# Two 256-token matmuls per weight tile in place of one of 512, in the gate and up projections of a two-block network

## The chip, the cores and the metric

The kernel runs on one core of one Trainium2 chip. The metric is the device time of one execution in microseconds (us); the median of three runs of the kernel before is 2926.17 us (2924.74 to 2929.9).

## The reference, cut to what matters

The reference is a two-block network on 512 tokens of width 1024, in fp32: feed-forward, a hybrid mixer (state-space and banded attention), feed-forward; then a gated-delta-rule mixer, feed-forward, a gated projection, a stick-breaking attention, feed-forward, a gated projection. The change touches the first two products of each of the four feed-forward layers:

```
D_MODEL, SEQ, D_FF = 1024, 512, 2816

def swiglu(h, w_gate, w_up, w_down):
    return (jax.nn.silu(h @ w_gate) * (h @ w_up)) @ w_down

# first block, twice (around its mixer)
x = x + 0.5 * swiglu(rms_norm(x, ffn_norm), w_gate, w_up, w_down)
# second block, twice (gate and up are the halves of one matrix)
h = h + swiglu_2(rms_norm_2(h, ln_ffn), ffn_w_in, ffn_w_out)
```

## The kernel before

Activations are kept transposed: features lie on the 128 partitions, the 512 tokens (T) along the free dimension, so x is 8 tiles (DK) of 128 x 512. Each fp32 product is made of three matmuls on operands split into a high and a low part of type fp32r: high weights by high x, high weights by low x, low weights by high x. The fourth, low by low, is left out.

Weights come in units of 128 x 1024. For a gate or up layer a unit holds the 8 weight tiles (128 x 128) that give one output tile of 128 features by 512 tokens. SyncE's queue loads the units one after another into `raw` (2 slots, L1787), ScalarE rounds each into `w_hi` (4 slots, L392), GpSimd subtracts to get `w_lo` (L1822), and TensorE uses it.

The code of the feed-forward layers on TensorE is `pe_ffn`. The 22 tiles of hidden features go in two halves of 12 and 10. For each half, `pe_column_layer` runs 24 or 20 units (gate and up in turn), each with 24 matmuls (L326 to L328, k over 8, three for each k) into one PSUM bank of 512 fp32 columns; then `pe_square_half` runs twice for the down projection (L351 to L353). So the gate and up projections are 44 units a feed-forward layer and 176 in all, 4224 matmuls. The same `pe_column_layer` also makes the mixers' projections, which share lines L326 to L328 but not the change: 2256 more matmuls.

The order of work is the program's: each engine runs its own list and waits on counting semaphores. A unit waits once, at its first matmul, for `w_lo` of the unit and for a free bank. In the first unit of a layer (j == 0) each k also waits for its `x_lo` tile, which VectorE writes (L418). `each` writes the first unit out, runs a loop of laps of four units with a jump back (L118), and writes the last ones out: with 24 units 1 + 5 laps of 4 + 3, with 20 units 1 + 4 laps of 4 + 3.

While a unit runs, VectorE takes the result of the unit before out of PSUM with the scale (L495, L497), makes the product with the activated gate (L500) and its low part (L502). ScalarE does the SiLU (L467) and `mid_hi` (L470).

A matmul instruction of fp32r shows in the trace as one weight load (LDWEIGHTS, engine PEld) and one matmul (MATMUL, PE). A matmul on plain fp32 operands, as the mixers have them, shows as two of each, called passes below.

Of the kernel before, what the change touches and what calls it, by code (L numbers as in the profile page):

```python
# [24 lines left out]
T = 512  # L25
NB = T // P
D = 1024
DK = D // P
# [80 lines left out]
def each(eng, count, body, first=0, begin=0):  # L109

    at, end = begin + first, begin + count
    for u in range(begin, at):
        body(0, u)
    laps = (end - at) // 4
    if laps >= 2:
        with eng.Fori(0, laps) as i:  # L118
            for j in range(at, at + 4):
                body(i, j)  # L120
        at += laps * 4
    for u in range(at, end):
        body(0, u)
# [41 lines left out]
def build(nc, units, x_t, p_t, vectors, constants, rel_table, out_t):  # L165
# [4 lines left out]
    def place(name, at, shape, dtype=F32):  # L170

        size = int(np.prod(shape[1:])) * 4
        assert base + at + size <= limit, (name, base + at + size, limit)
        return nc.alloc_sbuf_tensor_at(name, shape, dtype, offset=base + at)

    with ExitStack() as ctx:
# [8 lines left out]
        x_hi = place("x_hi", 56 * KB, [P, DK, T], F32R)  # L185
        x_lo = place("x_lo", 72 * KB, [P, DK, T], F32R)
# [87 lines left out]
        ps = ctx.enter_context(nc.psum_tensor("ps", [P, 8, T], F32))  # L274
# [34 lines left out]
        def pe_norm_sum(pe, w, bank):  # L309

            pe.wait_ge(s_sum, 8 * (w.norms + 1))
            nc.tensor.matmul(ps[:, bank, :], ones, sum_sq[:, :], start=True, stop=True).then_inc(s_msum, 1)

        def pe_column_layer(pe, w, count, after_first=None):
            n0, b0, g = w.column_layer(count)

            def body(i, j):
                u, slot = i * 4 + j, (n0 + j) % W_SLOTS
                pe.wait_ge(s_wlo, n0 + u + 1)
                pe.wait_ge(s_free, b0 + u + 1)  # L320
                for k in range(DK):
                    if j == 0:
                        pe.wait_ge(s_xlo, w.tiles - DK + k + 1)
                    hi, lo = w_hi[:, slot, k * P:(k + 1) * P], w_lo[:, slot, k * P:(k + 1) * P]
                    out = ps[:, 4 * g + j % 4, :]
                    nc.tensor.matmul(out, hi, x_hi[:, k, :], start=(k == 0), stop=False)  # L326
                    nc.tensor.matmul(out, hi, x_lo[:, k, :], start=False, stop=False)  # L327
                    last = nc.tensor.matmul(out, lo, x_hi[:, k, :], start=False, stop=(k == DK - 1))  # L328
                last.then_inc(s_used, 1)
                if j == 0 and after_first is not None:  # L330
                    after_first(4 * (g ^ 1))

            each(pe, count, body, first=1)

        def pe_square_half(pe, w, tiles, rhs, ready):

            n0, b0, g, prev, _ = w.square_layer(tiles // 2)
            for kp in range(tiles // 2):
                slot = (n0 + kp) % W_SLOTS
                pe.wait_ge(s_wlo, n0 + kp + 1)  # L340
                if kp == 0:
                    pe.wait_ge(s_free, prev + 4)
                for k2 in range(2):
                    k = 2 * kp + k2
                    ready(k)
                    r_hi, r_lo = rhs(k)
                    for m in range(4):
                        at = k2 * T + m * P
                        hi, lo = w_hi[:, slot, at:at + P], w_lo[:, slot, at:at + P]
                        out = ps[:, 4 * g + m, :]  # L350
                        nc.tensor.matmul(out, hi, r_hi, start=(k == 0), stop=False)  # L351
                        nc.tensor.matmul(out, hi, r_lo, start=False, stop=False)  # L352
                        last = nc.tensor.matmul(out, lo, r_hi, start=False, stop=(k == tiles - 1))  # L353
                        if k == tiles - 1 and m < 3:
                            last.then_inc(s_bank, 1)
                last.then_inc(s_used, 1)
# [82 lines left out]
        def pe_ffn(pe, w):  # L439
            for half, tiles in enumerate(HALVES):  # L440
                if half == 0:
                    w.tiles += DK
                    pe_column_layer(pe, w, 2 * tiles, lambda bank: pe_norm_sum(pe, w, bank))
                    w.norms += 1
                else:
                    pe_column_layer(pe, w, 2 * tiles)
                mids = w.mids
                for side in range(2):
                    pe_square_half(pe, w, tiles, lambda k: (mid_hi[:, k, :], mid_lo[:, k, :]),
                                   lambda k: pe.wait_ge(s_mlo, mids + k + 1))  # L450
                w.mids += tiles
# [183 lines left out]
        def pe_mixer1(pe, w):  # L635
            w.tiles += DK
            pe_column_layer(pe, w, U_END, lambda bank: pe_norm_sum(pe, w, bank))
            w.norms += 1
            pe_rstd_columns(pe, w)
# [1221 lines left out]
        @block.tensor  # L1861
        def _(pe):
            w = Walk()
            pe.wait_ge(s_const2, 16)
            pe_ffn(pe, w)
            pe_mixer1(pe, w)
            pe_ffn(pe, w)
            pe_final_norm(pe, w)
            pe_mixer2(pe, w)
            pe_ffn(pe, w)  # L1870
            pe_embed(pe, w)
            pe_mixer3(pe, w)
            pe_ffn(pe, w)
            pe_embed(pe, w)
            assert w.unit == NREAL, (w.unit, NREAL)
# [130 lines left out]
```

## Time and profile before

| | |
|---|---|
| median of 3 runs | 2926.17 us |
| lowest, highest | 2924.74, 2929.9 us |
| span of the profiled execution | 2923.0 us |
| weight loads and matmuls recorded | 12450 each |
| mean granted TensorE clock | 0.969 |

The profiled execution has no time of its own beside its span (first to last instruction). The median of the runs lies 3.2 us above that span; this is taken as what lies around it.

How to read the rows: the time shown for a matmul is from its start to its modelled end, and matmuls overlap, so neither the sum of durations nor the busy share tells the rate. The rate is the distance from one start to the next; it is called the pitch below.

### The profile page before, as it was taken

The page shows a single profiled execution, that of the slowest core. Times are in us where ns is not written, and L with a number is a line of the kernel's source. Part 1 is how long each engine was busy: PE and PEld are TensorE (multiplying, and loading weights), DVE is VectorE, ACT ScalarE, POOL GpSimd, SP SyncE. Part 2 cuts the span into 40 slices and gives each one's busy share as a digit, 9 for nine tenths or more (in the row PEclk, how much of TensorE's full clock was granted, in tenths as well). Part 3 has the DMA queues.
Part 4 walks back from the last instruction along what each step waited for, and adds up shares of the span by engine and source line. Part 5 has one row for each costly group of instructions (what it writes and reads, how often), then busy time and mean ns, then how long its engine had stood idle before and what let it go on. Part 6 is the DMA issues. An engine that isn't in the chain of part 4 may idle for free.

```text
span 2923.0 us, 35055 instructions
## 1 busy us (share of the span) xinstructions
PE 2758.2 (94%) x12450; PEld 2197.1 (75%) x12450; DVE 995.6 (34%) x1504; ACT 1029.6 (35%) x1475; POOL 1103.4 (38%) x522
## 2 busy tenths in 40 slices
PE   8999999979899999899888899999999989999998
PEld 6888888644788888676577678888778567888886
DVE  3212228347332121884433352112241322321224
ACT  4222333334342222424543442222342443422233
POOL 4444434300344444344322234444344402444443
PEclk9999999989999999999898999999999999999999
DMA  4333322300233333123000023333223101333333
GB/s 150 93 101 94 97 90 88 107 0 1 72 94 94 101 93 101 58 87 100 0 0 0 0 86 95 100 96 99 87 85 90 49 0 43 101 94 101 94 101 101
DMA packets 61691, 222.27 MB, mean 76 GB/s; under 512 B 6704, under 2 KB 6832, under 8 KB 61488
## 3 DMA queue, kind: packets, MB, share of 16 engines
q1 hardware_dynamic: 60928, 218.07, 24.5%
q10 hardware_dynamic: 688, 3.15, 0.3%
q8 instruction: 53, 0.87, 0.1%
q14 instruction: 22, 0.18, 0.0%
HBM read 219.09 MB, written 2.10 MB: 76 GB/s over the span
## 4 chain that ended last, share of the span: by engine, by line
PE 67%; issue 19%; POOL 7%; ACT 3%; DVE 3%; DMA 0%; POOLq 0%; ACTq 0%; SPq 0%; DVEq 0%
PE ps L326 12%; PE ps L328 12%; PE ps L327 12%; POOL w_lo L1822 7%; PE ps L351 5%; PE ps L352 5%; PE ps L353 5%; PE ps L1240 2%; PE ps L1605 2%; PE ps L1231 1%; PE ps L589 1%; PE ps L1092 1%; PE ps L372 1%; PE ps L374 1%; PE ps L373 1%
## 5 line engine op out<-in xcount | busy, mean ns | idle before, releaser
L1822 POOL TENSOR_TENSOR w_lo<-raw,w_hi 128x1024 fp32r<-128x1024 f32 x405 | 988.5, 2442 | 1436.6 <-ACT w_hi L392 1436.5
L326 PE MATMUL ps<-x_hi,w_hi 128*128 128x512 f32 x2160 | 850.4, 394 | 32.6 <-DVE x_lo L418 16.9
L328 PE MATMUL ps<-x_hi,w_lo 128*128 128x512 f32 x2160 | 842.6, 390 | 0.0
L327 PE MATMUL ps<-x_lo,w_hi 128*128 128x512 f32 x2160 | 842.6, 390 | 0.0
L392 ACT ACTIVATE w_hi<-raw 128x1024 fp32r<-128x1024 f32 x405 | 425.4, 1051 | 578.0 <-PE ps L353 360.7
L326 PEld LDWEIGHTS ps<-x_hi,w_hi 128*128 128x128 f32 x2160 | 406.7, 188 | 132.5 <-issue 26.7
L328 PEld LDWEIGHTS ps<-x_hi,w_lo 128*128 128x128 f32 x2160 | 406.6, 188 | 85.6
L327 PEld LDWEIGHTS ps<-x_lo,w_hi 128*128 128x128 f32 x2160 | 406.9, 188 | 85.2 <-issue 2.2
L351 PE MATMUL ps<-mid_hi,w_hi 128*128 128x512 f32 x960 | 377.4, 393 | 21.9 <-DVE mid_lo L1536 13.1
L352 PE MATMUL ps<-mid_lo,w_hi 128*128 128x512 f32 x960 | 375.8, 391 | 0.0
L353 PE MATMUL ps<-mid_hi,w_lo 128*128 128x512 f32 x960 | 375.5, 391 | 0.0
L517 DVE SCALAR_TENSOR_TENSOR h<-ps,h 128x512 f32<-128x512 f32 x88 | 60.2, 689 | 497.9 <-PE ps L353 497.9
L351 PEld LDWEIGHTS ps<-mid_hi,w_hi 128*128 128x128 f32 x960 | 181.9, 189 | 61.7 <-issue 24.0
L352 PEld LDWEIGHTS ps<-mid_lo,w_hi 128*128 128x128 f32 x960 | 181.8, 189 | 38.3 <-issue 0.5
L353 PEld LDWEIGHTS ps<-mid_hi,w_lo 128*128 128x128 f32 x960 | 181.6, 189 | 38.2
L497 DVE TENSOR_TENSOR ff_up<-ps,rstd 128x512 f32<-128x512 f32 x88 | 60.9, 692 | 406.9 <-PE ps L328 406.9
L470 ACT ACTIVATE mid_hi<-ff_up 128x512 f32 (+1 forms) x88 | 55.6, 632 | 390.7 <-DVE ff_up L500 390.7
L629 DVE SCALAR_TENSOR_TENSOR cv<-pad,vec,cv 128x512 f32<-128x512 f32 x108 | 146.1, 1353 | 15.7 <-DVE cv L629 0.3
L467 ACT ACTIVATE ff_gate<-ff_gate 128x512 f32<-128x512 f32 x88 | 55.6, 632 | 252.8 <-DVE ff_gate L495 252.7
L495 DVE TENSOR_TENSOR ff_gate<-ps,rstd 128x512 f32<-128x512 f32 x88 | 60.9, 692 | 223.6 <-PE ps L328 205.3
L1491 POOL TENSOR_TENSOR ao<-at,const 128x512 f32<-128x512 f32 x48 | 60.4, 1271 | 163.0 <-DVE tt L1435 111.5
L502 DVE TENSOR_TENSOR mid_lo<-ff_up,mid_hi 128x512 f32 x88 | 65.8, 748 | 80.9 <-ACT mid_hi L470 80.9
(268 smaller groups left out, 2456.8 us busy)
## 6 DMA issues: line engine op xcount, KB each, us to landing
raw<-in_units_dram SPq DMA_DIRECT2D x406, 512.0 KB, 3.6
h<-in_x_t_dram SPq DMA_DIRECT2D x4, 512.0 KB, 6.8
toep<-in_rel_table_dram ACTq DMA_DIRECT2D x1, 2048.0 KB, 9.1
out_dram<-h SPq DMA_DIRECT2D x4, 512.0 KB, 5.5
p_f<-in_p_t_dram ACTq DMA_DIRECT2D x2, 512.0 KB, 3.8
const<-in_constants_dram SPq DMA_DIRECT2D x1, 832.0 KB, 9.5
vec<-in_vectors_dram SPq DMA_DIRECT2D x1, 133.5 KB, 2.3
```

The source lines that it names most:

```text
L326: nc.tensor.matmul(out, hi, x_hi[:, k, :], start=(k == 0), stop=False)
L327: nc.tensor.matmul(out, hi, x_lo[:, k, :], start=False, stop=False)
L328: last = nc.tensor.matmul(out, lo, x_hi[:, k, :], start=False, stop=(k == DK - 1))
L351: nc.tensor.matmul(out, hi, r_hi, start=(k == 0), stop=False)
L352: nc.tensor.matmul(out, hi, r_lo, start=False, stop=False)
L353: last = nc.tensor.matmul(out, lo, r_hi, start=False, stop=(k == tiles - 1))
L392: nc.scalar.activation(w_hi[:, n % W_SLOTS, :], raw[:, n % RAW_SLOTS, :], ACT.Copy).then_inc(s_whi, 1)
L495: nc.vector.tensor_tensor(ff_gate[:, pair, :], ps[:, 4 * g + j % 4, :], rstd[:, :], ALU.mult).then_inc(s_free, 1)
L497: nc.vector.tensor_tensor(ff_up[:, pair, :], ps[:, 4 * g + j % 4, :], rstd[:, :], ALU.mult).then_inc(s_free, 1)
L502: nc.vector.tensor_tensor(tile_at(mid_lo, done), ff_up[:, pair, :], tile_at(mid_hi, done).bitcast(F32), ALU.subtract).then_inc(s_mlo, 1)
L629: last = nc.vector.scalar_tensor_tensor(out=cv[:, slot, :], in0=pad[:, slot, q:q + T], scalar=tap(q), in1=cv[:, slot, :], op0=ALU.mult, op ...
L1822: nc.gpsimd.tensor_tensor(w_lo[:, n % W_SLOTS, :], raw[:, n % RAW_SLOTS, :], w_hi[:, n % W_SLOTS, :].bitcast(F32), ALU.subtract).then_inc( ...
```

## The change

In `pe_column_layer`, where the new argument `token_halves` is true, a weight tile's three matmuls of 512 tokens become two sets of three matmuls of 256 tokens, the first on tokens 0 to 255 and the second on 256 to 511. Both write the same PSUM bank, each its own half. Only the very first matmul of a bank carries the start flag. `pe_ffn` passes true for both halves of all four feed-forward layers. No other engine's list changes.

```diff
-        def pe_column_layer(pe, w, count, after_first=None):
+        def pe_column_layer(pe, w, count, after_first=None, token_halves=False):
...
-                    out = ps[:, 4 * g + j % 4, :]
-                    nc.tensor.matmul(out, hi, x_hi[:, k, :], start=(k == 0), stop=False)
-                    nc.tensor.matmul(out, hi, x_lo[:, k, :], start=False, stop=False)
-                    last = nc.tensor.matmul(out, lo, x_hi[:, k, :], start=False, stop=(k == DK - 1))
+                    if not token_halves:
...
+                    else:
+                        for t in range(2):
+                            cols = slice(t * T // 2, (t + 1) * T // 2)
+                            out = ps[:, 4 * g + j % 4, cols]
+                            nc.tensor.matmul(out, hi, x_hi[:, k, cols], start=(k == 0 and t == 0), stop=False, skip_group_check=True)
+                            nc.tensor.matmul(out, hi, x_lo[:, k, cols], start=False, stop=False, skip_group_check=True)
+                            last = nc.tensor.matmul(out, lo, x_hi[:, k, cols], start=False, stop=(k == DK - 1), skip_group_check=True)
...
-                    pe_column_layer(pe, w, 2 * tiles, lambda bank: pe_norm_sum(pe, w, bank))
+                    pe_column_layer(pe, w, 2 * tiles, lambda bank: pe_norm_sum(pe, w, bank), True)
...
-                    pe_column_layer(pe, w, 2 * tiles)
+                    pe_column_layer(pe, w, 2 * tiles, None, True)
```

On TensorE, the first unit of the first feed-forward layer, k = 0 and the start of k = 1. Before:

```order
L326 MATMUL ps<-x_hi,w_hi 128x512 [waits banks_free,x_lo_ready,w_lo_ready,masks_loaded]
L327 MATMUL ps<-x_lo,w_hi 128x512
L328 MATMUL ps<-x_hi,w_lo 128x512
L326 MATMUL ps<-x_hi,w_hi 128x512 [waits x_lo_ready]
L327 MATMUL ps<-x_lo,w_hi 128x512
```

After:

```order
L334 MATMUL ps<-x_hi,w_hi 128x256 [waits banks_free,x_lo_ready,w_lo_ready,masks_loaded]
L335 MATMUL ps<-x_lo,w_hi 128x256
L336 MATMUL ps<-x_hi,w_lo 128x256
L334 MATMUL ps<-x_hi,w_hi 128x256
L335 MATMUL ps<-x_lo,w_hi 128x256
L336 MATMUL ps<-x_hi,w_lo 128x256
L334 MATMUL ps<-x_hi,w_hi 128x256 [waits x_lo_ready]
```

Between one wait for an `x_lo` tile and the next there were three matmuls, and there are six of half the width.

On TensorE, the end of a unit inside the loop and the start of the next (L319 counts the wait's value). Before:

```order
L326 MATMUL ps<-x_hi,w_hi 128x512
L327 MATMUL ps<-x_lo,w_hi 128x512
L328 MATMUL ps<-x_hi,w_lo 128x512
L319 REGISTER_ALU
L326 MATMUL ps<-x_hi,w_hi 128x512 [waits banks_free,w_lo_ready]
```

After:

```order
L334 MATMUL ps<-x_hi,w_hi 128x256
L335 MATMUL ps<-x_lo,w_hi 128x256
L336 MATMUL ps<-x_hi,w_lo 128x256
L319 REGISTER_ALU
L334 MATMUL ps<-x_hi,w_hi 128x256 [waits banks_free,w_lo_ready]
```

The waits stand at the same places; from one to the next there are 48 matmuls in place of 24, so a loop's body is 192 in place of 96.

## Rows read from the trace of the kernel before

**Rows 1.** The page: busy time, share of the span, instructions of each engine; granted clock.

```profile
span 2923.0 us, 35055 instructions
PE 2758.2 (94%) x12450; PEld 2197.1 (75%) x12450; DVE 995.6 (34%) x1504; ACT 1029.6 (35%) x1475; POOL 1103.4 (38%) x522
```

**Rows 2.** Windows: a gate-and-up layer of 20 units; busy us by engine.

```profile
core 0: us, PE busy (x) PEld busy (x) DVE busy (x) ACT busy (x) POOL busy (x), PEclk, DMA share, GB/s
1008.60:1117.40 108.80, 108.80 (x482) 90.09 (x481) 26.60 (x39) 31.12 (x39) 47.97 (x20) 1.00 0.31 96
```

**Rows 3.** Groups of the page: count, busy us, mean ns, idle time before and its releaser.

```profile
L326 PE MATMUL ps<-x_hi,w_hi 128*128 128x512 f32 x2160 | 850.4, 394 | 32.6 <-DVE x_lo L418 16.9
L328 PE MATMUL ps<-x_hi,w_lo 128*128 128x512 f32 x2160 | 842.6, 390 | 0.0
L326 PEld LDWEIGHTS ps<-x_hi,w_hi 128*128 128x128 f32 x2160 | 406.7, 188 | 132.5 <-issue 26.7
```

**Rows 4.** Timeline, a steady stretch of such a layer: start us, duration us, engine.

```profile
249.93 0.39 PE L327 MATMUL ps<-x_lo,w_hi 128*128 128x512 f32 x1
...
251.06 0.39 PE L326 MATMUL ps<-x_hi,w_hi 128*128 128x512 f32 x1
...
249.93 0.19 PEld L328 LDWEIGHTS ps<-x_hi,w_lo 128*128 128x128 f32 x1
250.16 0.19 PEld L326 LDWEIGHTS ps<-x_hi,w_hi 128*128 128x128 f32 x1
```

**Rows 5.** Timeline, the kernel's first matmuls, at the lower granted clock.

```profile
14.30 0.63 PE L328 MATMUL ps<-x_hi,w_lo 128*128 128x512 f32 x1
14.73 0.63 PE L326 MATMUL ps<-x_hi,w_hi 128*128 128x512 f32 x1
15.16 0.63 PE L327 MATMUL ps<-x_lo,w_hi 128*128 128x512 f32 x1
```

**Rows 6.** Timeline, mixers: plain fp32 passes of 384, 128, 256 and 512 columns.

```profile
2356.03 0.81 PE L1615 MATMUL ps<-sb_l,sb_v 128*128 128x384 f32 x2
2356.68 0.38 PE L1613 MATMUL ps<-sb_l,sb_v 128*128 128x128 f32 x2
2356.90 0.60 PE L1615 MATMUL ps<-sb_l,sb_v 128*128 128x256 f32 x2
2357.34 0.38 PE L1613 MATMUL ps<-sb_l,sb_v 128*128 128x128 f32 x2
...
1669.29 7.03 PE L1092 MATMUL ps<-nrm_sq,const 128*128 128x512 f32 x16
```

**Rows 7.** Timeline, weight loads of a stream of 128-column passes.

```profile
1473.09 0.30 PEld L1269 LDWEIGHTS ps<-qkt,vn 128*128 128x128 f32 x2
1473.32 0.30 PEld L1271 LDWEIGHTS ps<-vn,kd 128*128 128x128 f32 x2
1473.54 0.30 PEld L1267 LDWEIGHTS ps<-qd,st 128*128 128x128 f32 x2
```

**Rows 8.** Timeline, two of eight small transposes in a row, one instruction each.

```profile
643.75 0.21 PE L696 MATMUL ps<-const,cs_row 16*128 16x16 f32 x1
643.81 0.21 PE L697 MATMUL ps<-const,dt_row 16*128 16x16 f32 x1
```

**Rows 9.** Loads of one lap of the delta-rule loop; DMA queues from 1465 to 1680 us.

```profile
1486.00:1542.00 56.00, 45.41 (x374) 0.96 0.00 0
...
DMA packets 1, 0.01 MB, mean 0 GB/s; under 512 B 0, under 2 KB 0, under 8 KB 0
q14 instruction: 1, 0.01, 0.0%
```

**Rows 10.** First unit of a layer: TensorE's wait for x_lo; line L418's own durations.

```profile
816.59 0.50 PE L326 MATMUL ps<-x_hi,w_hi 128*128 128x512 f32 x1 [0.30 <-DVE x_lo L418]
L418 DVE SCALAR_TENSOR_TENSOR x_lo<-h,vec,x_hi x80: 735/747/2241, 8.2 to 2857.8; 128x512 fp32r<-128x512 f32 x80
```

More of the change, by code:

```diff
@@ L324, in body @@
                     hi, lo = w_hi[:, slot, k * P:(k + 1) * P], w_lo[:, slot, k * P:(k + 1) * P]
-                    out = ps[:, 4 * g + j % 4, :]
-                    nc.tensor.matmul(out, hi, x_hi[:, k, :], start=(k == 0), stop=False)
-                    nc.tensor.matmul(out, hi, x_lo[:, k, :], start=False, stop=False)
-                    last = nc.tensor.matmul(out, lo, x_hi[:, k, :], start=False, stop=(k == DK - 1))
+                    if not token_halves:
+                        out = ps[:, 4 * g + j % 4, :]
+                        nc.tensor.matmul(out, hi, x_hi[:, k, :], start=(k == 0), stop=False)
+                        nc.tensor.matmul(out, hi, x_lo[:, k, :], start=False, stop=False)
+                        last = nc.tensor.matmul(out, lo, x_hi[:, k, :], start=False, stop=(k == DK - 1))
+                    else:
[5 more added lines that the diff above has]
+                            last = nc.tensor.matmul(out, lo, x_hi[:, k, cols], start=False, stop=(k == DK - 1), skip_group_check=True)
                 last.then_inc(s_used, 1)
```

## The prediction

> **What bounds the kernel now.** I read the page first: TensorE is busy for 94% of the span, no other engine for more than 38% [rows 1]. A busy share of pipelined matmuls is not a rate, so the windows come next, cut to the layers that the change touches. A layer of 20 units holds 480 matmuls and takes 108.8 us, with TensorE busy in all of it, and the granted clock is 1.00, the 2.4 GHz level [rows 2]: 226.7 ns from start to start, 5.44 us a unit. The timeline shows the same in single rows: five matmuls from 249.93 to 251.06, 226 ns each [rows 4]. In that layer GpSimd, the busiest helper, works 48.0 us and ScalarE 31.1 us of 108.8 [rows 2], so weights are ready long before they are needed. In the groups, all 2160 matmuls of L326 are preceded by 32.6 us of idle time together, and L328 by none [rows 3]. TensorE's own pace sets the time here, and a nanosecond added to each matmul's pitch is a nanosecond on the end.
>
> **What a pitch is made of.** At 2.4 GHz one column per cycle, 512 columns are 213.3 ns. The pitch is 226.7, so 13.3 ns are something else. Three readings bear on what.
> - At the lower clock (0.5, 1.2 GHz) the same matmuls start 0.43 us apart [rows 5], and 512 columns are 426.7 ns there: nothing is left over. So the 13.3 ns are no gap in issuing that would show at either clock.
> - Plain fp32 passes run at 1.2 columns per ns. Two of 384 columns take 0.65 us (0.325 each, 320 for the columns), two of 256 take 0.44 (0.22; 213), two of 128 take 0.22 (0.11; 107), and sixteen of 512 take 7.03 us with the last one's drain, where their columns are 6.83, so at most 12 ns each are left [rows 6]. What is left of the narrower ones is 3 to 7 ns by rows rounded to 10 ns. One column in 17 lost would be 20 ns at 384 and 27 at 512: a part per pass, not a rate.
> - Each matmul has a weight load, which starts when the matmul before it starts and is shown as 0.19 us long [rows 4].
>
> **The change part by part.**
>
> *Columns.* 4224 matmuls of 512 become 8448 of 256: the same number of columns. At one column per cycle this part costs nothing.
>
> *The part per matmul.* If the 13.3 ns are paid once for each matmul and its load, a matmul of 256 has a pitch of 106.7 + 13.3 = 120.0 ns. The gate and up layers take 8448 x 120.0 = 1013.8 us in place of 4224 x 226.7 = 957.4: +56.3 us. Before has no fp32r matmul narrower than 512, so this cost must be bounded. Below: if the 13.3 ns are a rate (one column in 17 lost), 256 columns take 113.3 ns and the change costs nothing; and if they go altogether, the next limit is the weight load. Loads of 128 columns start 0.22 us apart for two, that is 111 to 112 ns [rows 7]; 8448 x 111.7 = 943.6 us, -13.8 us. Above: if the 13.3 ns come on top of the load's own 111.7, the pitch is 125.0 and the cost +98.6 us. I take 120.0, because the plain fp32 rows, the nearest with several widths, have a remainder that is the same at every width, and because the load is the same size at each width: whatever it takes from the moving operand, it takes once a load.
>
> *The loads.* They double, from 4224 to 8448. Today a load has 226.7 ns to hide in, in future about 120. The row at issue is the shown length, 188 ns [rows 3], longer than the new pitch. But loads of 0.19 us each follow each other every 0.11 us under the 128-column passes, two of them within 0.30 [rows 7]. So the shown length is latency, loads overlap each other, and the cover of 120 ns is enough, by 8 ns. That margin is thin, and it is why the range goes up to the case above.
>
> The Trainium skill's page "Perfetto Trace Analysis", section "Identifying the Most-Contended Engine", advises judging TensorE by LDWEIGHTS busy share, summed slice time over the window. By that rule the layer of 20 units is at 90.1 of 108.8 us, 83%, and doubled loads want 180 us: the load would become the bound. The trace speaks against it, since 374 loads of 0.19 us, 71 us by their sum, stood in 45.4 us of busy time within one lap of the delta-rule loop [rows 9].
>
> *Issuing.* Twice as many instructions go through TensorE's sequencer in the same time, one every 120 ns. Small transposes, one instruction each, start 0.06 us apart [rows 8], so issuing hides with a factor of two.
>
> *The loop's body.* It grows from 96 to 192 load-and-matmul pairs. The delta-rule loop's laps have 374 loads, and over its second to fourth lap TensorE's instruction queue moves nothing (the one packet is of q14, another queue) [rows 9]. A body twice as long as the new one is held, so a jump back costs nothing.
>
> The skill's page "Runtime: NRT & Kernel Launch", section "Instruction fetch mechanics", says that a taken branch beyond a window of two pages of code forces a fetch. The same row speaks against it for a body of this size.
>
> *The first units.* There each k waits for x_lo, which VectorE makes in some 0.75 us a tile, and TensorE idles, 0.30 us in the case shown [rows 10]. Six matmuls of 120.0 take 0.72 us where three took 0.68, so part of the 0.32 us that a first unit grows by is taken from this idle time: at most 1.3 us over four layers, which I leave at 0.5 given back. The kernel's first matmuls run at the lower clock, where two of 256 should take what one of 512 takes, since nothing is left over there [rows 5].
>
> *Other engines and memory.* Nothing is added on VectorE, ScalarE, GpSimd or SyncE. A unit lengthens from 5.44 to 5.76 us, which gives them slack. Three matmuls running add onto the same 256 columns, 120 ns apart; the two passes of a 128-column product add onto the same columns 110 ns apart without a stall [rows 6]. The bank is released after the unit's last matmul, as before.
>
> *Sum.* 2923.0 + 56.3 - 0.5 = 2978.8 us of span; with 3.2 us around it, by the distance of the median from this span, 2982.0 us, +1.9%.
>
> **The rivals.**
>
> *The extra is a rate, or goes (not slower).* Pitch 113.3 down to 111.7: 2926 down to 2912 us. For it: the lower clock shows no extra at all [rows 5], as would be if the moving operand's supply were just short of 2.4 columns per ns; that is a rate. Against it: a shortage of supply would also be expected from a load that shares it, which is once per load. The point at which it decides is a pitch of 113.3; below it the kernel is faster than before, and it is faster by over 0.2% only below 112.6.
>
> *Part of it is a rate (slower, less).* The plain passes pay 3 to 7 ns each whatever their width; if fp32r pays 3 of that kind and the other 10.3 are a rate, 256 columns have 106.7 + 5.2 + 3 = 114.9 ns, +13 us, 2939 us. For it, that the plain passes, with the same loads, pay no more; against it, that a load then costs fp32r nothing beyond what it costs them.
>
> The skill's page "TensorE: Matmul & The Clock Gate", section "Back-to-back issue gap", gives 262 cycles for 256 columns and 518 for 512, 109.2 and 215.8 ns at 2.4 GHz, so the change would add 11 us by it, close to this rival. The trace disagrees on 512 columns, 226.7 ns.
>
> *The load becomes the bound (slower).* The 107 ns of columns no longer cover a load of 111.7 ns, and the 13.3 come on top: 125.0 ns, 2926.2 + 98.6 = 3025 us. For it: the margin is 8 ns, and no row shows loads this dense beside a moving operand at full rate. Against: then loads would have to be slowed by what slows the matmul.
>
> *Loads don't overlap with fp32r* (188 ns each as shown): 8448 x 188 = 1588 us, +631, 3557 us. Against it rows 7, though those are passes of plain fp32.
>
> *The narrow matmul loses the full rate* and runs as plain fp32 does, 216 ns for 256: 1825 us, +867, 3794 us. Nothing in the trace shows it, nor excludes it.
>
> *Code is fetched again at each jump back.* There are 28 of them (four layers by 4 + 3). The waits put down to issue before L326's loads are 26.7 us in all [rows 3]; as many again would give 3009 us. Against it rows 9.
>
> **How the numbers follow.** Chances: forecast 0.54; extra is a rate or goes 0.15 (0.06 of it under 2920); part of it a rate 0.08; load as the bound 0.12; code fetch 0.03; loads in full 0.04; full rate lost 0.04. The range goes from 2920 to 3040 us: from the rate case up to a pitch of 126.8. It leaves out the two large cases and the lower end of the first rival. A measurement of this kernel can tell 0.2% from no change, 6 us, a pitch of 112.6 to 114.0. Faster 0.06, same 0.09, slower 0.85.
>
> **What would show it.** In the profile after, a layer of 20 units should take 115.2 us where it took 108.8 and hold 960 loads, with starts 120 ns apart in the timeline. The remainder after 106.7 ns is the answer: 13.3 for the forecast, 6.6 for a rate, 8.2 for part of it a rate, 18 for the load as the bound, 81 for loads in full. A load's shown length should stay near 0.19 us. The down projections should keep 226.7 ns, and the instruction queue should have no more packets during the loops. Idle time before the first matmul of a unit, once in each lap, would mean code fetch. If the clock row falls below 1.00 in these layers, or GpSimd's w_lo shows as a releaser there, the prediction's basis is wrong.

## The result and the profile after

The changed kernel takes 2982.81 us (median of 4 runs, 2979.36 to 2985.56), the kernel before 2927.94 in the same measurement; the ratio on record is 1.0192, with a 95% interval of 1.0175 to 1.021 (the two medians by themselves give 1.0187). The profiled execution has a span of 2977.5 us, 54.5 more than before. The page of the changed kernel, with the gate and up matmuls now on L334 to L336:

```profile
span 2977.5 us, 43503 instructions
PE 2812.8 (94%) x16674; PEld 2418.7 (81%) x16674; DVE 999.3 (34%) x1504; ACT 1029.8 (35%) x1475; POOL 1103.6 (37%) x522
...
q8 instruction: 65, 1.06, 0.1%
...
L334 PE MATMUL ps<-x_hi,w_hi 128*128 128x256 f32 x2816 | 799.6, 284 | 13.9 <-DMA const<-in_constants_dram 13.2
L335 PE MATMUL ps<-x_lo,w_hi 128*128 128x256 f32 x2816 | 797.4, 283 | 0.0
```

There are 16674 - 12450 = 4224 more matmuls, as many as were cut in two, and TensorE waits before L334 for 13.9 us in all, 13.2 of it for the first load of constants, and before L335 for nothing. Its busy share is 94% as before, so this share says nothing about the pace.

The windows of the changed kernel, a layer of 24 units and one of 20 (answering to [rows 2]):

```profile
core 0: us, PE busy (x) PEld busy (x) DVE busy (x) ACT busy (x) POOL busy (x), PEclk, DMA share, GB/s
824.60:964.30 139.70, 139.46 (x1156) 138.74 (x1156) 39.43 (x55) 46.30 (x59) 57.58 (x24) 1.00 0.27 90
1029.50:1144.80 115.30, 115.30 (x962) 115.26 (x961) 26.55 (x39) 31.10 (x39) 48.01 (x20) 1.00 0.27 91
```

The layer of 20 units went from 108.8 to 115.2 us, taken from its first start to the first start behind it (the window is 0.1 longer), with the clock at 1.00 in both, and DVE, ACT and POOL do the same work in it. Its 960 matmuls and loads are 120 ns apart, as the timeline (answering to [rows 4]; start us, duration us, engine) shows row by row:

```profile
1080.05 0.28 PE L335 MATMUL ps<-x_lo,w_hi 128*128 128x256 f32 x1
1080.17 0.28 PE L336 MATMUL ps<-x_hi,w_lo 128*128 128x256 f32 x1
1080.29 0.28 PE L334 MATMUL ps<-x_hi,w_hi 128*128 128x256 f32 x1
...
1080.05 0.19 PEld L336 LDWEIGHTS ps<-x_hi,w_lo 128*128 128x128 f32 x1
1080.17 0.19 PEld L334 LDWEIGHTS ps<-x_hi,w_hi 128*128 128x128 f32 x1
```

256 columns at 2.4 per ns are 106.7 ns, so 13.3 ns are left, exactly what was left of 226.7 at 512 columns. The loads, 0.19 us long, now overlap each other (PEld busy 115.26 of 115.30 us), and that does no harm.

### The profile page after: what moved, and what is told of

Read it like the earlier page. It is cut to its first block, busy times and chain, and to the rows that moved or that the text cites. A ratio compares the mean times of both kernels' runs of the same rounds, so it can differ in the third digit from the quotient of the medians.

```text
span 2977.5 us, 43503 instructions
## 1 busy us (share of the span) xinstructions
PE 2812.8 (94%) x16674; PEld 2418.7 (81%) x16674; DVE 999.3 (34%) x1504; ACT 1029.8 (35%) x1475; POOL 1103.6 (37%) x522
## 4 chain that ended last, share of the span: by engine, by line
PE 67%; issue 19%; POOL 6%; DVE 3%; ACT 3%; DMA 0%; POOLq 0%; SPq 0%; ACTq 0%; DVEq 0%
PE ps L334 8%; PE ps L336 8%; PE ps L335 8%; POOL w_lo L1830 6%; PE ps L359 5%; PE ps L360 5%; PE ps L361 5%; PE ps L327 4%; PE ps L329 4%; PE ps L328 4%; PE ps L1248 2%; PE ps L1613 2%; PE ps L1239 1%; PE ps L597 1%; PE ps L1100 1%
## 5 line engine op out<-in xcount | busy, mean ns | idle before, releaser
L334 PE MATMUL ps<-x_hi,w_hi 128*128 128x256 f32 x2816 | 799.6, 284 | 13.9 <-DMA const<-in_constants_dram 13.2
L335 PE MATMUL ps<-x_lo,w_hi 128*128 128x256 f32 x2816 | 797.4, 283 | 0.0
L336 PE MATMUL ps<-x_hi,w_lo 128*128 128x256 f32 x2816 | 797.4, 283 | 0.0
L334 PEld LDWEIGHTS ps<-x_hi,w_hi 128*128 128x128 f32 x2816 | 541.2, 192 | 15.8 <-DMA const<-in_constants_dram 13.2
L335 PEld LDWEIGHTS ps<-x_lo,w_hi 128*128 128x128 f32 x2816 | 541.3, 192 | 1.2 <-issue 1.0
L336 PEld LDWEIGHTS ps<-x_hi,w_lo 128*128 128x128 f32 x2816 | 541.1, 192 | 0.0
L327 PE MATMUL ps<-x_hi,w_hi 128*128 128x512 f32 x752 | 299.5, 398 | 18.3 <-DVE x_lo L426 15.9
L328 PE MATMUL ps<-x_lo,w_hi 128*128 128x512 f32 x752 | 294.3, 391 | 0.0
L329 PE MATMUL ps<-x_hi,w_lo 128*128 128x512 f32 x752 | 294.2, 391 | 0.0
L327 PEld LDWEIGHTS ps<-x_hi,w_hi 128*128 128x128 f32 x752 | 142.1, 189 | 60.7 <-issue 25.7
L329 PEld LDWEIGHTS ps<-x_hi,w_lo 128*128 128x128 f32 x752 | 142.1, 189 | 30.0
```

Of the source, the lines that this page charges most:

```text
L334: nc.tensor.matmul(out, hi, x_hi[:, k, cols], start=(k == 0 and t == 0), stop=False, skip_group_check=True)
L335: nc.tensor.matmul(out, hi, x_lo[:, k, cols], start=False, stop=False, skip_group_check=True)
L336: last = nc.tensor.matmul(out, lo, x_hi[:, k, cols], start=False, stop=(k == DK - 1), skip_group_check=True)
```

## The experiments

The rows fixed the size of the cost at once. Open was whether it is what the sum took it for, one part per matmul, and when the weight load takes over. Edits are against the changed kernel. "Before" in each text is the kernel before.

**Half of the layers.** A dose and a test of even spread.

```diff
-                    pe_column_layer(pe, w, 2 * tiles, None, True)
+                    pe_column_layer(pe, w, 2 * tiles)
```

> The gate and up layers of 24 units use 256-token matmuls, those of 20 units keep 512. Theory (13.3 ns once for each fp32r matmul and its load, pitch 120.0): 96 units of 24 matmuls split, 2304 x (240.0 - 226.7) = +30.7 us over the kernel before, ratio 1.0105; the 24-unit layers' unit 5.76 us, the 20-unit layers' 5.44 us. Rival (something paid once for each layer, stage or jump back, such as code fetch or a late wait, that only happens to sum to 56 us): by jumps back 16 of 28, +32 us, but then as gaps in the timeline and not as an even pitch; by layers, half, +28 us.

Measured: 2958.95 us against 2925.39 for the kernel before on the same chip, ratio 1.0107 (1.009 to 1.0124), where 1.0105 was expected. The windows, a layer of 24 units and one of 20:

```profile
core 0: us, PE busy (x), PEclk, DMA share, GB/s
824.20:964.00 139.80, 139.55 (x1157) 1.00 0.28 90
1029.30:1138.20 108.90, 108.90 (x482) 1.00 0.30 96
```

The split layer has the changed kernel's time and the other has that of before, so the cost sits inside the split layers. The total can't tell the two theories apart (+30.7 or +28 to +32 us): by the medians it grew by 33.6 us, and the four runs lie from 2952.55 to 2960.85. The pitch does: the starts in the split layers are 120.0 ns apart, and no gap recurs at the laps. The rival of something paid per lap or per layer falls.

**The same weight twice in a row.** Is the part for exchanging one tile for another?

```diff
-                        for t in range(2):
-                            cols = slice(t * T // 2, (t + 1) * T // 2)
-                            out = ps[:, 4 * g + j % 4, cols]
-                            nc.tensor.matmul(out, hi, x_hi[:, k, cols], ...)
-                            nc.tensor.matmul(out, hi, x_lo[:, k, cols], ...)
-                            last = nc.tensor.matmul(out, lo, x_hi[:, k, cols], ...)
+                        halves = [slice(t * T // 2, (t + 1) * T // 2) for t in range(2)]
+                        bank = 4 * g + j % 4
+                        for t, cols in enumerate(halves):
+                            nc.tensor.matmul(ps[:, bank, cols], hi, x_hi[:, k, cols], ...)
+                        for cols in halves:
+                            nc.tensor.matmul(ps[:, bank, cols], hi, x_lo[:, k, cols], ...)
+                        for cols in halves:
+                            last = nc.tensor.matmul(ps[:, bank, cols], lo, x_hi[:, k, cols], ...)
```

> Halves as in the changed kernel, but the two token halves of one weight tile stand directly behind each other (high by x_hi on both halves, high by x_lo on both, low by x_hi on both), so each load but the first of a pair brings what the array already holds. Theory (once per matmul, whatever is loaded): pitch 120.0 everywhere, the time of the changed kernel, 2982 us, ratio to before 1.019. Rival (the part is for exchanging one weight tile for another): the second of each pair costs 2.5 to 3 ns in place of 13.3, so 4224 x 10.8 = 45 us are given back, ratio 1.004.

Measured: 2982.12 us, ratio 1.0194 (1.0177 to 1.0211). Timeline, two matmuls to a row:

```profile
1080.05 0.40 PE L336 MATMUL ps<-x_lo,w_hi 128*128 128x256 f32 x2
1080.29 0.40 PE L338 MATMUL ps<-x_hi,w_lo 128*128 128x256 f32 x2
```

0.24 us for two, with a load for each (the page of this run has 16674 loads, as many as matmuls). Whether a load brings a new tile or the same one doesn't matter, and the order within a k neither.

**The down projections too.** Does the part hold in a layer with another order of banks?

```diff
-                        out = ps[:, 4 * g + m, :]
-                        nc.tensor.matmul(out, hi, r_hi, start=(k == 0), stop=False)
...
+                        for t in range(2):
+                            cols = slice(t * T // 2, (t + 1) * T // 2)
+                            out = ps[:, 4 * g + m, cols]
+                            nc.tensor.matmul(out, hi, r_hi[:, cols], start=(k == 0 and t == 0), stop=False, skip_group_check=True)
...
```

> The down projections of the four feed-forward layers, and the mixers' output projections made by the same function, use 256-token matmuls too: 2880 more matmuls of 512 become 5760 of 256. Theory: 2880 x 13.3 = +38.4 us over the changed kernel, 2927.9 + 56.3 + 38.4 - 0.5 = 3022 us, ratio 1.0322. Rival (the 120 ns belong to the column layers alone, where one bank is written for 48 matmuls; the down projection goes round four banks): nothing added, 1.019, or another pitch, up to the load-bound 125, 1.042.

Measured: 3017.84 us, ratio 1.0316 (1.0299 to 1.0333). Over the changed kernel that is 35.0 us by the medians and 37.1 by the spans of the profiled executions (3014.6 and 2977.5), where 38.4 were expected. The two down projections behind a layer of 20 units in a window of this kernel:

```profile
1162.00:1219.60 57.60, 57.60 (x482) 1.00 0.31 94
```

Their 480 matmuls take 57.5 us from first start to last: the pitch is the same 120. The rival that the 120 ns belong to the column layers falls. In the two traces the stretches that were split here grew by 37.9 us together, 0.5 less than 38.4. The rest of what is missing lies within the spread of the runs, 2 us for this kernel and 6 us for the changed one.

**Quarters.** Where does the load become the bound? The slice is a quarter, and t runs over four.

```diff
-                        for t in range(2):
-                            cols = slice(t * T // 2, (t + 1) * T // 2)
+                        cuts = (0, 128, 256, 384, 512)
+                        for t in range(len(cuts) - 1):
+                            cols = slice(cuts[t], cuts[t + 1])
```

> Each weight tile is used for four sets of matmuls of 128 tokens in the gate and up layers, 16896 matmuls in place of 4224. This asks where the weight load becomes the bound. Theory (13.3 per matmul on the columns' time, loads beside it with a floor of 111.7 as the plain passes show): 53.3 + 13.3 = 66.7 is below the floor, so pitch 111.7, 16896 x 111.7 = 1887 us for the layers, +930 us, 3857 us. Rival (the part comes on top of whichever is longer): pitch 125, +1154 us, 4082 us. Rival (loads go faster when the matmul does): pitch 66.7 to 111, from +169 us, 3097 us.

Measured: 3862.87 us (one run) against the 3857 of the theory. A window over a layer of 20 units:

```profile
1376.70:1591.10 214.40, 214.40 (x1922) 214.39 (x1920) 26.51 (x39) 31.05 (x39) 47.44 (x20) 1.00 0.17 51
```

214.4 us for 1920 matmuls is 111.7 ns each, with 53.3 ns of columns in it. This is the pace at which loads follow each other in [rows 7] too. The 13.3 ns don't come on top of it, so the rival of 125 ns falls. In the changed kernel the 120 ns lie above this floor. That the floor is the load's is a reading. For it, the next experiment has loads 0.11 us apart where two matmuls start 0.06 apart. It is no floor of every 4-byte load of 128 columns: those of the small transposes, on 16 partitions, follow each other faster in the kernel before (their matmuls are in [rows 8]), and are shown shorter:

```profile
643.78 0.14 PEld L697 LDWEIGHTS ps<-const,dt_row 16*128 16x128 f32 x1
643.84 0.14 PEld L696 LDWEIGHTS ps<-const,cs_row 16*128 16x128 f32 x1
```

**Unequal parts.** 384 tokens, then 128, by `cuts = (0, 384, 512)`.

> Each weight tile is used for 384 tokens and then for 128, in the gate and up layers. Theory (pitch is the columns' time plus 13.3, or the floor that a weight load sets, 111.7, where that is longer): 384 columns 160 + 13.3 = 173.3, 128 columns 111.7, together 285.0 for what took 226.7, 4224 x 58.3 = +246 us, 3174 us. Rival (the matmul's and the load's parts trade off over several matmuls, since loads run ahead during the wide ones): 173.3 + 66.7 = 240, the same time as the changed kernel, 2982 us. The matmul behind which the long pitch stands tells in which one's time the load lies.

Measured: 3178.19 us (one run), where 3174 was expected. The timeline of one k:

```profile
1199.92 0.39 PE L335 MATMUL ps<-x_hi,w_hi 128*128 128x384 f32 x1
1200.15 0.34 PE L336 MATMUL ps<-x_lo,w_hi 128*128 128x384 f32 x1
1200.32 0.34 PE L337 MATMUL ps<-x_hi,w_lo 128*128 128x384 f32 x1
1200.50 0.22 PE L335 MATMUL ps<-x_hi,w_hi 128*128 128x128 f32 x1
1200.56 0.27 PE L336 MATMUL ps<-x_lo,w_hi 128*128 128x128 f32 x1
1200.67 0.27 PE L337 MATMUL ps<-x_hi,w_lo 128*128 128x128 f32 x1
1200.78 0.40 PE L335 MATMUL ps<-x_hi,w_hi 128*128 128x384 f32 x1
...
1200.33 0.19 PEld L335 LDWEIGHTS ps<-x_hi,w_hi 128*128 128x128 f32 x1
1200.50 0.19 PEld L336 LDWEIGHTS ps<-x_lo,w_hi 128*128 128x128 f32 x1
1200.61 0.19 PEld L337 LDWEIGHTS ps<-x_hi,w_lo 128*128 128x128 f32 x1
1200.72 0.19 PEld L335 LDWEIGHTS ps<-x_hi,w_hi 128*128 128x128 f32 x1
1200.83 0.19 PEld L336 LDWEIGHTS ps<-x_lo,w_hi 128*128 128x128 f32 x1
```

Six matmuls take 0.86 us (0.855 expected), so the part and the floor are not averaged over several matmuls, and the rival of 240 ns for a pair falls. The single rows need care. The load of the first narrow matmul starts at 1200.33, beside the last wide one. The load of the second starts only with the first, at 1200.50, and still the second is shown 0.06 later. But it is shown as 0.27 us long, where the first is 0.22, and the 384 at 1200.78 as 0.40 in place of 0.34. So it seems that a matmul whose load is late is shown from before the load is in, and that the wait is part of its shown time; then the gaps of 0.06 and 0.23 are not costs of their own. In the rows a load never starts earlier than the matmul before its own.

**Narrower loads.** Is the part a share of the load's columns? Here the matmuls have 512 tokens again.

```diff
...
+                        out = ps[:, 4 * g + j % 4, :]
+                        nc.tensor.matmul(out, hi, x_hi[:, k, :], start=(k == 0), stop=False, skip_group_check=True)
+                        nc.tensor.matmul(out[0:64], hi[:, 0:64], x_lo[:, k, :], start=False, stop=False, skip_group_check=True)
+                        last = nc.tensor.matmul(out[0:32], lo[:, 0:32], x_hi[:, k, :], start=False, stop=(k == DK - 1), skip_group_check=True)
```

> 512-token matmuls as in the kernel before, but in the gate and up layers the second product (high by x_lo) is made for 64 of the 128 features of a tile only and the third (low by x_hi) for 32; the low parts of the others are left out. So the weight loads of a k are 128, 64 and 32 columns wide. Theory A (the 13.3 ns are taken by the load from the moving operand in proportion to the columns loaded): the matmul beside the 64-column load is at 213.3 + 2.5 + 5.4, beside the 32-column one at 213.3 + 2.5 + 2.7, 16 ns less a k, 1408 x 13.5 = -19 us against before. Theory B (fixed per load or matmul whatever its width): 226.7 throughout, the time of before.

Measured: 2939.44 us (one run) against 2929.59 of before, slower than either theory. Timeline:

```profile
1050.24 0.39 PE L332 MATMUL ps<-x_hi,w_hi 128*128 128x512 f32 x1
1050.47 0.39 PE L333 MATMUL ps<-x_lo,w_hi 128*64 128x512 f32 x1
1050.70 0.40 PE L334 MATMUL ps<-x_hi,w_lo 128*32 128x512 f32 x1
1050.93 0.39 PE L332 MATMUL ps<-x_hi,w_hi 128*128 128x512 f32 x1
...
1050.24 0.14 PEld L333 LDWEIGHTS ps<-x_lo,w_hi 128*64 128x64 f32 x1
1050.47 0.11 PEld L334 LDWEIGHTS ps<-x_hi,w_lo 128*32 128x32 f32 x1
```

The loads are shown shorter (0.14, 0.11 us), but all starts are 0.23 apart, 231 ns on average in place of 226.7. So a shorter load gives nothing back, which speaks against the load taking turns with the moving operand column by column. (The pitches that the text above gives for theory A save 13.6 ns a k, not 16.) The two matmuls with narrower loads also write fewer partitions of PSUM, so two things changed at once, and why this costs 4 ns more a matmul is open.

**Two readings with bf16.** Both operands of the gate and up matmuls are read as the upper 16 bits of the same tiles, a stride of 4 bytes.

```diff
+                        def top(ap):
+                            return ap.bitcast(mybir.dt.bfloat16)[:, 1::2]
...
+                        nc.tensor.matmul(out, top(hi), top(x_hi[:, k, :]), start=(k == 0), stop=False)
...
```

> 512-token matmuls as in the kernel before, but in the gate and up layers both operands are read as the upper 16 bits of the same tiles, as bf16; the lower bits of the operands are left out. Theory (the 13.3 ns belong to 4-byte operands at the full column rate): pitch 213.3 + about 2.5 = 216, as the remainder of the plain passes, 4224 x -10.8 = -46 us against before, 2882 us. Rival (once per load and matmul whatever the type): 226.7, 2928 us.

> The same bf16 reading (lower bits left out) with 256-token matmuls. Theory (types decide the part): 106.7 + 2.5 = 109.2 if the load keeps up, 8448 x 109.2 = 922 us for the layers, -35 us against before, 2893 us; 111.7 if a load of 128 columns is still the floor, -14 us. Rival (once per load and matmul whatever the type): 120.0, 2983 us.

Measured: 2922.91 and 2929.77 us (one run each) against 2929.59. At 512 the starts are 225.0 ns apart, at 256 113.3, so neither theory holds: what is left beside the columns, 11.7 and 6.7 ns, grows with the width. In this form the halves are almost free, 1.7 ns a pair, where fp32r pays 13.3.

**All widths.** Each of the eight gate-and-up layers is a stream of one width of fp32r; a table replaces the halves.

```diff
+        LAYERS = [(512, (0,)), (448, (0, 64)), (384, (0, 128)), (320, (0, 192)), (288, (0, 224)), (256, (0, 256)), (240, (0, 136, 272)), (224, (0, 144, 288))]
...
+                        width, starts = kind
+                        for t, at in enumerate(starts):
+                            cols = slice(at, at + width)
```

> The eight gate-and-up layers, in the order in which they run, use fp32r matmuls of 512, 448, 384, 320, 288, 256, 240 and 224 tokens, in one, two or three sets that together cover the 512 tokens; where sets overlap, tokens are added twice, so the values there are not the reference's. Each layer is thus a stream of one width. Theory (columns at 2.4 per ns plus 13.3 ns a matmul, not under the load's floor of 111.6 that the 128-token run showed): pitches 226.7, 200.0, 173.3, 146.7, 133.3, 120.0, 113.3, 111.6; +331 us against before, 3259 us. Rival (the part is a rate, one column in 17, and the 120.0 at 256 is the load's doing): 226.7, 198.3, 170.0, 141.7, 127.5, 120.0, 111.6 to 120, 111.6 to 120; +311 us or more, 3239 us.

Measured: 3257.99 us (one run); the theory had 3259. The windows from the layer of 448 to that of 224:

```profile
213.20:407.80 194.60, 194.60 (x961) 180.34 (x961) 26.54 (x39) 31.11 (x39) 47.99 (x20) 1.00 0.17 57
899.20:1099.60 200.40, 200.40 (x1155) 199.92 (x1154) 37.01 (x55) 46.03 (x58) 57.33 (x24) 1.00 0.20 65
1164.90:1305.70 140.80, 140.80 (x961) 140.76 (x960) 26.53 (x39) 31.11 (x39) 48.27 (x20) 1.00 0.23 76
1917.70:2072.10 154.40, 154.40 (x1156) 153.92 (x1155) 38.69 (x55) 46.10 (x59) 57.61 (x24) 1.00 0.26 85
2137.40:2252.60 115.20, 115.20 (x962) 115.20 (x961) 26.50 (x39) 31.30 (x39) 47.92 (x20) 1.00 0.27 90
2709.70:2905.20 195.50, 195.50 (x1732) 194.98 (x1732) 37.17 (x55) 46.22 (x59) 57.38 (x24) 1.00 0.21 69
2970.50:3131.30 160.80, 160.80 (x1442) 160.80 (x1441) 26.47 (x39) 31.15 (x39) 47.79 (x20) 1.00 0.21 69
```

| columns | matmuls | pitch measured, ns | columns' time, ns | left, ns |
|---|---|---|---|---|
| 448 | 960 | 202.7 | 186.7 | 16.0 |
| 384 | 1152 | 173.3 | 160.0 | 13.3 |
| 320 | 960 | 146.7 | 133.3 | 13.3 |
| 288 | 1152 | 133.3 | 120.0 | 13.3 |
| 256 | 960 | 120.0 | 106.7 | 13.3 |
| 240 | 1728 | 112.6 | 100.0 | 12.6 |
| 224 | 1440 | 111.7 | 93.3 | 18.4 |

The pitch is the mean distance between starts within the layer, the first unit aside. At 256, 288, 320, 384 and 512 columns the same 13.3 ns are left: a part per matmul. A rate would have left 10.0 at 384 and 7.5 at 288. At 224 the load's floor of 111.7 is reached. Two widths don't fit: 240 takes 0.7 ns less than the 113.3 of the theory, and 448 takes 2.7 ns more than its 200.0. Both are unexplained. In the total they partly cancel (2.6 us more, 1.3 us less), so its agreement within 1 us is closer than the theory deserves.

**Which operand bf16 pays for.** The eight layers differ in what is packed (2 bytes from element to element): both operands, the moving one alone, or the load alone. Packed operands come from a constant tile.

```diff
+        LAYERS = [("bf16", "packed", "packed", 512), ("bf16", "packed", "packed", 256), ("bf16", "packed", "strided", 512), ("bf16", "packed", "strided", 256), ("bf16", "strided", "packed", 512), ("bf16", "strided", "packed", 256), ("bf16", "packed", "packed", 128), ("bf16", "packed", "strided", 128)]
...
+                        dtype, moving, loaded, width = kind
```

> The gate-and-up layers read bf16 operands, in the order: moving operand packed (2 bytes from one element to the next, from a constant tile) with a packed load, 512 and 256 columns; moving packed with the load taken at a stride of 4 bytes from the weights, 512 and 256; moving operand at a stride of 4 bytes from x with a packed load, 512 and 256; moving packed, 128 columns, packed load, then strided load. The products of these layers are thereby replaced by others of the same shapes. Known before: strided both, 225.0 at 512 and 113.3 at 256, so 225.0 = 213.3 + 11.7 and 113.3 = 106.7 + 6.7. Theory (the remainder comes from reading 4 bytes a column at the full rate on the moving side): packed moving 215.8 and 109.2 whatever the load is, strided moving 225.0 and 113.3. Rival (it comes from the load's reading): packed load 215.8 and 109.2 whatever the moving operand is, strided load 225.0 and 113.3. At 128 columns a load's shown 0.10 us in place of 0.19 should let the pitch fall under 111.6, to between 56 and 96.

Measured: 2903.2 us (one run) against 2926.15. The windows (weight loads) with the moving operand packed and the load strided, 256 columns; moving strided and load packed, 256; moving packed and load strided, 128:

```profile
core 0: us, PEld busy (x), PEclk, DMA share, GB/s
994.60:1099.50 104.90, 93.94 (x961) 1.00 0.30 100
1909.20:2018.10 108.90, 91.89 (x962) 1.00 0.29 96
2669.80:2777.10 107.30, 107.25 (x1921) 1.00 0.30 98
```

109.2, 113.3 and 55.8 ns from start to start; at 512 columns it is 215.8 (moving packed) and 225.8 (moving strided). The moving operand's stride decides, whatever the load reads, as the theory had it. And a bf16 load of 128 columns is no bound even at 55.8 ns, half the floor of an fp32r load.

## Why the prediction was right, point by point

**The bound.** "TensorE's own pace sets the time here" held: the helper engines' work in a 20-unit layer is unchanged, and the layer grew by what its matmuls grew.

**The part per matmul**, the term that carries the sum, was taken at 13.3 ns and measured 13.3: 120.0 ns, where the bounds were 111.7 and 125.0. From first start to the first start behind the layer, each of 20 units went from 108.80 to 115.19 us, +6.39, where 480 x 13.33 is 6.40. The reason given, the even remainder of the plain fp32 passes, pointed the right way, and the streams of several widths show it for fp32r itself. The second reason, that the load takes something from the moving operand once, is not shown: narrower loads gave nothing back, and packed bf16 matmuls with a 128-column load each leave only 2.5 ns. The argument from the load was a guess that agreed with the right number.

**The loads.** The cover of 120 ns was enough, by 8.3: the floor is 111.7 in the run with quarters. The row at issue, a shown length of 0.19 us, set no pace: loads shown that long follow each other every 0.12 us. The rule of LDWEIGHTS busy share, the summed time of the loads over the window (the Trainium skill, page "Perfetto Trace Analysis", section "Identifying the Most-Contended Engine"), would put the changed layer past its limit: 961 loads of 0.19 us are 183 us in 115.3. The trace disagrees: some load is shown running in nearly all of the window in the changed layer (115.26 of 115.30 us) and in those from 384 down to 224 columns alike, and their pitches go from 173.3 to 111.7 ns.

**Issuing and the loop's body** cost nothing, as said. The longest gap between starts in a layer of 20 units is 0.12 us, so neither issuing nor a jump back shows. The instruction queue moves no packet from 845 to 945 us, within the laps of a layer of 24 units. In the whole program it has 65 where it had 53; 12 more packets of 16 KB are the code of the 1536 matmuls that are written out more, 128 bytes for each with its load. Fetching a body again at each of 28 jumps would have been 28 x 192 x 128 bytes, an estimate of 42 packets more.

**The first units.** The wait for the last x_lo shrank (the idle time shown from 0.30 us [rows 10] to 0.24). The starts of before and of the changed kernel at that place, answering to [rows 10]:

```profile
815.90 0.40 PE L328 MATMUL ps<-x_hi,w_lo 128*128 128x512 f32 x1
816.59 0.50 PE L326 MATMUL ps<-x_hi,w_hi 128*128 128x512 f32 x1 [0.30 <-DVE x_lo L418]
...
829.56 0.28 PE L336 MATMUL ps<-x_hi,w_lo 128*128 128x256 f32 x1
830.08 0.39 PE L334 MATMUL ps<-x_hi,w_hi 128*128 128x256 f32 x1 [0.24 <-DVE x_lo L426]
```

0.69 us became 0.52, though the even pitch is 0.23 in the one and 0.12 in the other. From its first start to that of the second unit, this unit took 6.70 us before and 6.71 now.

This was the one term that was mis-sized. The layers of 24 units went from 132.26 to 139.58 us, +7.32 (the first from 133.06 to 140.48, +7.42), where 576 x 13.33 is 7.68. So 0.36 are given back in each of three and 0.26 in the first, 1.3 us in all: the upper end that the step named, where 0.5 was taken. In the three, a first unit's whole growth of 0.32 us goes into its waits, and a little more. The first layer is another case: its starts show no wait for x_lo. There the first matmuls run at the lower clock, as the step said:

```profile
13.59 0.41 PE L335 MATMUL ps<-x_lo,w_hi 128*128 128x256 f32 x1
13.81 0.41 PE L336 MATMUL ps<-x_hi,w_lo 128*128 128x256 f32 x1
```

Two of 256 columns, 0.21 us apart, take the 0.43 us of one of 512 [rows 5]. Seven matmuls of 512 ran at that clock in the kernel before, so this explains some 0.1 of the 0.26; the rest was not followed up.

**The sum.** The eight layers grew by 4 x 6.39 + 3 x 7.32 + 7.42 = 54.9 us, and the span by 54.5 (55.8 were forecast). Of the 1.3 us between forecast and span, 0.8 are the first units, and 0.4 lie in unchanged stretches and were not followed up. That the time came out within 1 us of 2982.0 is partly luck. The span fell 1.3 us short, but the median lies 5.3 us above the span of the profiled execution, where the sum added 3.2. Each run of the changed kernel lies only 1.9 us above its own span; the rest is that the profiled one was the fastest of the four. So the 3.2 was not "what lies around" the span. The difference of the medians, 54.9 where 55.8 was forecast, is the fairer test.

**The rivals.** A rate, and a part of it a rate: excluded for fp32r by the table. The load as the bound, loads that don't overlap, and the loss of the full rate: excluded by 120.0 ns at 256 columns. Even half that width runs at 111.7. Code fetch: excluded by the even pitch.

## What to carry to other kernels

Read a matmul stream by the distance of its starts, take off the columns at the granted clock, and treat what is left as paid once for each fp32r matmul: 13.3 ns here (16.0 at 448 columns), so an fp32r weight tile should meet as many tokens in one matmul as the bank holds. The share of time lost is 6% at 512 columns and 11% at 256; at 224 and 128 columns the 128-column fp32r load sets 111.7 ns, and from the two figures the crossing can be estimated at 236 columns. Neither the order of the halves nor repeating a weight tile gets any of it back.

## What the runs showed of the hardware that had not been expected

- The 13.3 ns of fp32r don't shrink with the width of the load (128, 64 and 32 columns in turn gave 231 ns in place of 226.7), and they don't depend on whether the weight changes (120.0 either way). What they are for is open: every fp32r matmul here brought its load, so the matmul's part and the load's could not be told apart.
- bf16 with a packed moving operand leaves 2.5 ns at 512 and 256 columns (215.8 and 109.2), as the Trainium skill's page "TensorE: Matmul & The Clock Gate", section "Back-to-back issue gap", states for isolated gaps; with a 4-byte stride it leaves 11.7 to 12.5 at 512 (225.0 and 225.8) and 6.7 at 256 (113.3), a part that grows with the columns, unlike fp32r's.
- A bf16 load of 128 columns hides under a pitch of 55.8 ns; with an fp32r load of 128 columns no stream here went below 111.7.
- Loads run ahead by one matmul and no further: with 384 and 128 columns in turn a load starts with or after the matmul before its own, and six matmuls take 0.86 us, as three wide pitches and three floors do. The shown starts of matmuls behind a late load are not to be read one by one (0.06 and 0.23 us there).
